# A decoder block with 32 experts on one core: expert weights fetched in 4 MB transfers, 32 KB a partition, in place of 2 MB ones

## Chip, core and metric

The kernel runs on 1 core of a Trainium2 chip. The metric is device time in microseconds (us). Before the change, three runs took 1339.52 us (median), 1335.58 and 1339.84 us.

## What is computed

A block of 256 tokens of 1024 float32 features passes two mixers (a state-space scan and a sparse attention), a merge and a projection, and then a layer of 32 experts, of which each token uses its best four. The kernel computes all of it in float32. Cut to what matters here:

```python
def moe_ffn(h, router_w, router_b, w_gate_up, b_gate_up, w_down, b_down):
    t = h.reshape(256, 1024)
    combine = ...                                  # 256 x 32, four nonzero a row
    out = jnp.zeros_like(t)
    for e in range(32):
        a = clamped_swiglu(t @ w_gate_up[e] + b_gate_up[e])     # 1024 x 2048, 8 MB
        out = out + combine[:, e:e + 1] * (a @ w_down[e] + b_down[e])   # 1024 x 1024, 4 MB
    return out
```

An expert has 12 MB of weights, all 32 have 384 MB (402.65 million bytes), and each byte is read once.

## The kernel before

The first 400 us compute the mixers, the projection and the router. Their weights pass through the first four 8 KB slots of a tile `ring`; when they are done, the whole of `ring` (12 slots of 8 KB a partition) goes to the experts.

**The experts on TensorE.** For every expert the tokens that chose it (64 places) are gathered, multiplied by the gate and up weights, activated, turned, multiplied by the down weights and added back. Two experts make a pair, and two pairs a pass of the loop `Fori`. `odd_half` and `even_half` (L1099, L1122) write out the order of one half each:

- `gather(n)` (L1026 to L1035): for two experts at once, 8 blocks of 128 features by 2 halves of the tokens, with a 128x128 piece of the tile `H2` as the stationary operand and the selection matrix `SPR` as the moving one. Each float32 matmul is two records in the trace, so that a gather has 32 (line L1032). There is one gather a pair, 16 in all.
- `gate_up(s, j, slot, loads_n)` (L1037): unit j of 4 of the gate and up weights, 256 rows, 2 MB. It waits for its transfer and counts `unit_done` at its end. Its matmuls are 16 records at L1043.
- `act_turned(n)` (L1061): four 128x128 transposes of the activations `ABU` (name `HT` in the trace, since it lies in that tile; line L711). 32 in all, one an expert.
- `down(j, slot, loads_n)` (L1048): unit j of 2 of the down weights, 512 rows, 2 MB, 16 records at L1057.
- `combine(n, s)` (L1076, matmuls at L1083) spreads the results back over the tokens, `bias(s)` (L1014) starts an accumulation, and `weights_turned` turns the combining weights (L711, `QT`), once a pair.

The order is G(e+1), then D(e): down of an expert follows gate and up of the next. After G(31) and D(30) there is no more to overlap with: the kernel ends with `combine`, `act_turned` for expert 31, its two down units, `combine`, a norm and the store.

Which rows of a weight matrix a partition holds is fixed by the transfer. A unit of 256 rows goes in as `(p k) n -> p (k n)` with k=2: partition p gets rows 2p and 2p+1, one run of 16 KB. TensorE must therefore take the features of `H2` in the same order, every second one, and so it does in the stationary operand:

```python
first = 256 * (k // 2) + k % 2
ins = mm(bank(5 + k // 4, P, off=P * (k % 4)), H2[:, t, first:first + 255:2],
         SPR[:, t].rearrange("p a b -> p (a b)"), start=(t == 0), stop=(t == T - 1))
```

`act_turned` takes every second column of `ABU` likewise.

**The transfers.** SyncE's queue (SP) issues all of them, in the order of use, through `load_gu` (L501) and `load_dn`. There are 8 places of 16 KB a partition (`places`, L283): two outside `ring` (`slot0`, `slot1`), six in it. A ninth, `once`, is used for one unit alone. A place is loaded again when the unit in it has been multiplied: SP waits for `unit_done`. The first eight or nine transfers are issued one by one as the memory comes free from the mixers (L531 to L547); from then on each waits for the place that the unit 8 before it had.

Of the kernel before, what the change touches and what calls it, by code (L numbers as in the profile page):

```python
# [33 lines left out]
P = 128  # L34
D = 1024
# [18 lines left out]
BIG = 2 * SLOT  # L54
SLOTS = 8
# [3 lines left out]
ONCE = SLOTS  # L59
FIRST_SLOT = (0, 1, 2, ONCE)  # L60
LOOP_SLOT = tuple((n + 3) % SLOTS for n in range(PERIOD))
# [115 lines left out]
def hybrid_block(nc, x, mix_norm_w, w_in, conv_w, conv_b, dt_bias, a_log, d_skip, ssm_norm_w,  # L177
# [3 lines left out]
    with ExitStack() as ctx:  # L181
# [21 lines left out]
        def at_place(name, shape, place, dt=F32R):  # L203
# [149 lines left out]
        slot_full = [sem(f"slot_full{i}") for i in range(SLOTS + 1)]  # L353
# [93 lines left out]
        def loop_loads(i, pos):  # L447

            slot = LOOP_SLOT[pos]
            before = LOOP_SLOT[:pos].count(slot) + FIRST_SLOT.count(slot)  # L450
            return i * (16 * LOOP_SLOT.count(slot)) + 16 * (before + 1)
# [10 lines left out]
        def _(sp):  # L462
# [38 lines left out]
            def load_gu(e, j, slot):  # L501

                src = w_gate_up[0, e, 256 * j:256 * j + 256, :].rearrange("(p k) n -> p (k n)", k=2)
                sp.dma_start(places[slot], src).then_inc(slot_full[slot], 16)

            def load_dn(e, j, slot):

                src = w_down[0, e, 512 * j:512 * j + 512, :].rearrange("(p k) n -> p (k n)", k=4)
                sp.dma_start(places[slot], src).then_inc(slot_full[slot], 16)

            def load_at(pos, e, nxt, slot):

                h, n = pos // PAIR, pos % PAIR
                if n < 4:
                    load_gu(e + (2 * h + 1), n, slot)
                elif n < 6:
                    load_dn(e + 2 * h, n - 4, slot)
                elif n < 10:
                    load_gu(nxt if h else e + 2, n - 6, slot)
                else:  # L520
                    load_dn(e + (2 * h + 1), n - 10, slot)

            def first_load(n):

                if n < GU_U:
                    load_gu(0, n, FIRST_SLOT[n])
                else:
                    load_at(n - GU_U, 0, 4, LOOP_SLOT[n - GU_U])

            sp.wait_ge(pv_read, 16)  # L530
            first_load(0)  # L531
            sp.wait_ge(unit_done, at_unit[("bs", 3)] + 1)
            first_load(1)
            sp.wait_ge(unit_done, at_unit[("bn", 3)] + 1)
            first_load(2)
            low_ready(sp, len(SPLIT_UNITS) - 3)
            low_ready(sp, len(SPLIT_UNITS) - 2)
            first_load(4)
            sp.wait_ge(unit_done, at_unit[("wo", 1)] + 1)
            first_load(5)  # L540
            low_ready(sp, len(SPLIT_UNITS) - 4)
            low_ready(sp, len(SPLIT_UNITS) - 1)
            first_load(6)
# [17 lines left out]
            for n, pos in enumerate((*range(PAIR + 6), PERIOD - 2, PERIOD - 1)):  # L561
                sp.wait_ge(unit_done, units_to(last * 2, n - SLOTS + 1))
                load_at(pos, EXPERTS - 4, 0, LOOP_SLOT[n])
# [143 lines left out]
        def _(pe):  # L707
# [329 lines left out]
            def gate_up(s, j, slot, loads_n):  # L1037

                pe.wait_ge(slot_full[slot], loads_n)
                w = places[slot]  # L1040
# [7 lines left out]
            def down(j, slot, loads_n):  # L1048

                pe.wait_ge(slot_full[slot], loads_n)  # L1050
                w = places[slot]
                for hf in range(2):
                    for k in range(2):
                        lhs = ATS[:, 2 * j + k, 64 * hf:64 * hf + 64]
                        for h in range(2):
                            at = 2048 * k + 1024 * hf + 512 * h
                            ins = mm(psum[64 * h:64 * h + 64, 2, :], lhs, w[:, at:at + 512],  # L1057
                                     start=(j + hf + k == 0), stop=(j == 1 and hf + k == 2))
# [29 lines left out]
            for j in range(GU_U):  # L1088
                pe.wait_ge(xte_ready, 1 if j < 2 else 2)
                gate_up(0, j, FIRST_SLOT[j], 16)  # L1090
# [879 lines left out]
```

## Time and profile before

| | us |
|---|---|
| three runs | 1335.58, 1339.52, 1339.84 |
| the profiled execution, its own time | 1334.48 |
| its span in the trace | 1332.8 |
| TensorE busy | 1234.6 (93%) |
| chain that ended last, transfers of expert weights | 31% of the span |
| a 2 MB expert transfer, from issue to landing | about 34 |

The profile lists for every engine its records with start and length. "PE" are the matmuls of TensorE, "PEld" its loads of the stationary operand, which overlap the matmuls. "Busy" counts overlapping records once. The chain of waits goes back from the last instruction to what released it each time; a row in it that names DMA means that the work after it waited for a transfer. The granted clock of TensorE is 1.00 (2.4 GHz) in all of the expert stage behind its first microseconds.

### The profile page before, as it was taken

Reading aid. Unit: us, or ns where it says so; the run is one execution under the profiler, and the core shown is the slowest. Engines: PE = TensorE matmul, PEld = TensorE weight load, DVE = VectorE, ACT = ScalarE, POOL = GpSimd, SP = SyncE. Lnnn points to the kernel's source line nnn. Section 1 sums busy time; section 2 is a strip of 40 time slices with the busy share of each in tenths; the row PEclk is TensorE's granted clock in tenths of the full one; section 3 lists DMA queues with packets and bytes.
Section 4 is the critical chain, followed back from the end, with each engine's and each line's share of the span. In section 5 each row is a group of like instructions: output and inputs, shape, how many; then the busy total and the mean of one; then the engine's idle time right before and its main releaser. Section 6 shows DMA issues by size and latency. Waiting matters only on the chain.

```text
span 1332.8 us, 17482 instructions
## 1 busy us (share of the span) xinstructions
PE 1234.6 (93%) x7089; PEld 661.9 (50%) x7089; DVE 444.1 (33%) x902; ACT 282.3 (21%) x507; POOL 149.0 (11%) x101
## 2 busy tenths in 40 slices
PE   7999996898899999999999898998989899898985
PEld 7999986777884443434434233332423333232321
DVE  6965446455633131221212213121221212122113
ACT  4673444453331010101101011010101001010001
POOL 1301345353630000000000000000000000000000
PEclk9999997899999999999999999999999999999998
DMA  7747433112698999999999999999999999999994
GB/s 239 209 129 228 127 106 116 64 64 95 236 363 342 395 432 426 430 427 430 427 430 427 428 428 428 430 427 430 427 430 427 431 427 430 427 428 429 426 428 205
DMA packets 79964, 454.08 MB, mean 341 GB/s; under 512 B 10160, under 2 KB 53296, under 8 KB 55344
## 3 DMA queue, kind: packets, MB, share of 16 engines
q1 hardware_dynamic: 76960, 451.30, 82.9%
q10 hardware_dynamic: 2960, 2.17, 0.6%
q8 instruction: 31, 0.51, 0.2%
q14 instruction: 13, 0.11, 0.0%
HBM read 452.40 MB, written 1.05 MB: 340 GB/s over the span
## 4 chain that ended last, share of the span: by engine, by line
PE 60%; DMA 31%; DVE 6%; ACT 1%; issue 1%; ACTq 1%; POOL 0%; DVEq 0%; SPq 0%
DMA ring<-in_w_gate_up_dram 28%; PE psum L1043 19%; PE psum L1057 10%; PE psum L757 9%; PE psum L760 7%; PE psum L1032 5%; PE psum L1083 3%; DMA ring<-in_w_down_dram 3%; PE psum L711 2%; DVE AMX L1754 1%; PE psum L930 1%; DVE YV L1706 1%; DVE WL L1472 1%; PE psum L967 1%; PE psum L1014 1%
## 5 line engine op out<-in xcount | busy, mean ns | idle before, releaser
L1043 PE MATMUL psum<-ring,ZS 128*64 128x512 f32 x1504 | 355.2, 616 | 14.2 <-DMA ring<-in_w_gate_up_dram 14.2
L1043 PEld LDWEIGHTS psum<-ring,ZS 128*64 128x64 f32 x1504 | 100.0, 134 | 230.3 <-issue 192.5
L1906 DVE TENSOR_TENSOR X<-X,psum 128x1024 f32<-128x1024 f32 x64 | 75.3, 1217 | 388.7 <-PE psum L1083 388.7
L1057 PE MATMUL psum<-ring,HT 128*64 128x512 f32 x784 | 176.6, 596 | 20.3 <-DMA ring<-in_w_down_dram 19.6
L1890 DVE TENSOR_SCALAR ZS<-psum 128x512 f32<-128x512 f32 x32 | 22.1, 692 | 315.1 <-PE psum L1043 315.1
L1043 PE MATMUL psum<-slot,ZS 128*64 128x512 f32 x528 | 123.8, 615 | 2.0 <-DMA slot<-in_w_gate_up_dram 2.0
L1057 PEld LDWEIGHTS psum<-ring,HT 128*64 128x64 f32 x784 | 54.4, 136 | 129.9 <-issue 104.0
L1391 ACT ACTIVATE HT<-psum 128x512 f32<-128x512 f32 x32 | 19.1, 597 | 324.3 <-PE psum L711 324.3
L1472 DVE TENSOR_TENSOR WL<-ring,WH 128x2048 fp32r<-128x2048 f32 (+1 forms) x30 | 71.2, 2377 | 46.0 <-ACT WH L1184 46.0
L1184 ACT ACTIVATE WH<-ring 128x2048 fp32r<-128x2048 f32 (+1 forms) x42 | 78.5, 1873 | 10.2 <-issue 6.1
L1043 PEld LDWEIGHTS psum<-slot,ZS 128*64 128x64 f32 x528 | 35.6, 134 | 73.3 <-issue 64.7
L1032 PEld LDWEIGHTS psum<-QT,XC 128*128 128x128 f32 x512 | 63.0, 200 | 14.4 <-issue 14.4
L1032 PE MATMUL psum<-QT,XC 128*128 128x128 f32 x512 | 66.0, 289 | 1.5 <-DVEq L1829 1.5
L1083 PE MATMUL psum<-HT,QT 64*128 64x512 f32 x264 | 65.6, 615 | 1.6 <-ACT HT L1395 1.6
L1395 ACT ACTIVATE HT<-psum 128x512 f32<-128x512 f32 x32 | 19.1, 597 | 222.3 <-PE psum L1057 222.3
L621 POOL TENSOR_TENSOR WL<-ring,WH 128x2048 fp32r<-128x2048 f32 x12 | 55.2, 4603 | 41.2 <-ACT WH L1184 41.2
L1057 PE MATMUL psum<-slot,HT 128*64 128x512 f32 x240 | 54.3, 594 | 5.8 <-DMA slot<-in_w_down_dram 5.8
L1387 ACT ACTIVATE ZS<-ZS 128x512 f32<-128x512 f32 x32 | 20.2, 630 | 136.0 <-DVE ZS L1890 136.0
L757 PE MATMUL psum<-HTH,WH 128*128 128x256 f32 x320 | 47.5, 292 | 0.0
L757 PE MATMUL psum<-HTL,WH 128*128 128x256 f32 x320 | 46.2, 287 | 0.3 <-DVE HTL L1485 0.3
L757 PE MATMUL psum<-HTH,WL 128*128 128x256 f32 x320 | 45.4, 285 | 0.0
L1083 PEld LDWEIGHTS psum<-HT,QT 64*128 64x128 f32 x264 | 22.7, 186 | 45.4 <-issue 45.4
(322 smaller groups left out, 1306.6 us busy)
## 6 DMA issues: line engine op xcount, KB each, us to landing
ring<-in_w_gate_up_dram SPq DMA_DIRECT2D x94, 2048.0 KB, 33.8
ring<-in_w_down_dram SPq DMA_DIRECT2D x49, 2048.0 KB, 35.1
slot<-in_w_gate_up_dram SPq DMA_DIRECT2D x33, 2048.0 KB, 33.7
ring<-in_w_in_dram SPq DMA_DIRECT2D x30, 1024.0 KB, 5.5
slot<-in_w_down_dram SPq DMA_DIRECT2D x15, 2048.0 KB, 35.0
ring<-in_w_branch_ssm_dram SPq DMA_DIRECT2D x4, 1024.0 KB, 4.9
ring<-in_w_branch_nsa_dram SPq DMA_DIRECT2D x4, 1024.0 KB, 5.0
ring<-in_w_out_dram SPq DMA_DIRECT2D x4, 1024.0 KB, 4.9
```

The source lines that it names most:

```text
L621: g.tensor_tensor(WL[i % SPLITS][:], slot_view(k, SLOT), WHF[i % SPLITS], ALU.subtract).then_inc(wl_pool, 1)
L711: return nc.tensor.transpose(o, i, IDN[:, :])
L757: ins = mm(bank(b, 2, SEQ)[:, half], w[:, k, rows], src[:, k, :], start=(n == 0 and k == 0), stop=(n == 2 and k == KT - 1))
L760: ins = mm(bank(b, 2, nco)[:, half], src[:, k, rows], w[:, k, :], start=(n == 0 and k == 0), stop=(n == 2 and k == KT - 1))
L1032: ins = mm(bank(5 + k // 4, P, off=P * (k % 4)), H2[:, t, first:first + 255:2], SPR[:, t].rearrange("p a b -> p (a b)"), start=(t == 0), s ...
L1043: ins = mm(psum[64 * (c % 2):64 * (c % 2) + 64, c // 2, :], XTS[:, k, s], every_other_pair(w[:, 2048 * (k % 2):2048 * (k % 2) + 2048], c), ...
L1057: ins = mm(psum[64 * h:64 * h + 64, 2, :], lhs, w[:, at:at + 512], start=(j + hf + k == 0), stop=(j == 1 and hf + k == 2))
L1083: ins = mm(psum[:, 3 + 2 * t + h, :], CTS[r, s, t], YSB[r, :], start=True, stop=True)
L1184: a(WH[i % SPLITS][:, 0:n], slot_view(u, n), ACT.Copy).then_inc(wh_ready, 1)
L1472: v.tensor_tensor(WL[i % SPLITS][:, 0:n], slot_view(u, n), WHF[i % SPLITS][:, 0:n], ALU.subtract).then_inc(wl_ready, 1)
L1890: v.tensor_scalar(GBU.rearrange("p (q f) -> p q f", q=2), gu[:, :, :, 0], 7.0, None, ALU.min).then_inc(g_ready, 1)
L1906: v.tensor_tensor(xo, xo, psum[:, 3 + 2 * t:5 + 2 * t, :], ALU.add).then_inc(o_read, 1)
```

## The change

Two units become one transfer: 512 rows of gate and up weights, or all 1024 rows of a down matrix, each 4 MB, with 32 KB in one run for a partition (k=4 and k=8 in `(p k) n -> p (k n)`). The eight places of 16 KB become four of 32 KB on the same bytes. TensorE still works unit by unit and counts `unit_done` for each, but waits for a transfer ahead of every second unit, and SP waits with a transfer until both units of the old content are done. The first transfers, which go into memory that comes free piece by piece, and the down weights of the last expert stay 2 MB (`load_half`). Of the first ones, the transfer into `once` now goes ahead of one into the last free half place, and what was the first half of D(0) there is the first loaded half of G(2).

Since a partition now holds four neighbouring rows of gate and up weights, `gather` takes every fourth feature of `H2`; since it holds eight of the down weights, `act_turned` takes every fourth column of `ABU`.

```diff
-BIG = 2 * SLOT
-SLOTS = 8
+BIG = 4 * SLOT
+HALF = BIG // 2
+SLOTS = 4
-FIRST_SLOT = (0, 1, 2, ONCE)
-LOOP_SLOT = tuple((n + 3) % SLOTS for n in range(PERIOD))
+UNITS_4 = PERIOD // 2
+FIRST_SLOT = (0,)
+LOOP_SLOT = tuple((n + 2) % SLOTS for n in range(UNITS_4))
...
-        places = [at_place("slot0", [P, BIG], xdt_at + 4 * D, F32)[:],
-                  at_place("slot1", [P, BIG], ec_at, F32)[:]]
-        places += [part(ring, i * SLOT, BIG) for i in (4, 2, 8, 0, 10, 6)]
-        places += [at_place("once", [P, BIG], xc_at + 4 * 2048, F32)[:]]
+        places = [at_place("slot0", [P, BIG], xdt_at + 4 * D, F32)[:]]
+        places += [part(ring, i * SLOT, BIG) for i in (4, 0, 8)]
+        once = at_place("once", [P, HALF], xc_at + 4 * 2048, F32)[:]
...
+            def gate_up_rows(e, ab):
+
+                return w_gate_up[0, e, 512 * ab:512 * ab + 512, :].rearrange("(p k) n -> p (k n)", k=4)
+
+            def down_rows(e):
+
+                return w_down[0, e].rearrange("(p k) n -> p (k n)", k=8)
+
+            def load_half(rows, hi, to, full):
+
+                sp.dma_start(to, rows[:, HALF * hi:HALF * hi + HALF]).then_inc(full, 16)
...
             sp.wait_ge(unit_done, at_unit[("wo", 2)] + 1)
-            first_load(7)
-            sp.wait_ge(unit_done, NU)
-            first_load(8)
+            load_half(gate_up_rows(1, 1), 1, half_place(3, 1), slot_full[3])
             sp.wait_ge(bias_ready, 1)
             sp.wait_ge(rt_full, 1)
             sp.wait_ge(h2_ready, 4)
-            first_load(3)
-            for n in range(9, GU_U + PERIOD):
-                before = max(q for q in range(n) if (FIRST_SLOT + LOOP_SLOT)[q] == (FIRST_SLOT + LOOP_SLOT)[n])
-                sp.wait_ge(unit_done, NU + before + 1)
-                first_load(n)
+            load_half(gate_up_rows(0, 1), 1, once, part_full["once"])
+            sp.wait_ge(unit_done, NU)
+            load_half(gate_up_rows(2, 0), 1, half_place(1, 1), part_full["G2a"])
+            sp.wait_ge(unit_done, NU + 1)
+            load_half(down_rows(0), 0, half_place(0, 0), part_full["D0"])
+            sp.wait_ge(unit_done, NU + 2)
+            load_half(down_rows(0), 1, half_place(0, 1), slot_full[0])
+            sp.wait_ge(unit_done, NU + 3)
+            load_half(gate_up_rows(2, 0), 0, half_place(1, 0), slot_full[1])
+            sp.wait_ge(unit_done, NU + 5)
+            load_half(gate_up_rows(2, 1), 0, half_place(2, 0), slot_full[2])
...
+            for unit in range(5, UNITS_4):
+                sp.wait_ge(unit_done, units_to(0, 2 * unit - 6))
+                load_at(unit, 0, 4, LOOP_SLOT[unit])
             last = rounds(sp)
             with sp.Fori(1, last) as i:
-                for pos in range(PERIOD):
-                    sp.wait_ge(unit_done, units_to(i * 2, pos - SLOTS + 1))
-                    load_at(pos, (i % EX4) * 4, ((i + 1) % EX4) * 4, LOOP_SLOT[pos])
+                for unit in range(UNITS_4):
+                    sp.wait_ge(unit_done, units_to(i * 2, 2 * unit - 6))
+                    load_at(unit, (i % EX4) * 4, ((i + 1) % EX4) * 4, LOOP_SLOT[unit])
...
+            for hi in range(2):
+                sp.wait_ge(unit_done, units_to(last * 2, 11 + hi))
+                load_half(down_rows(EXPERTS - 1), hi, half_place(LOOP_SLOT[9], hi),
+                          slot_full[LOOP_SLOT[9]] if hi else part_full["last"])
...
                 for k in range(KT):
                     for t in range(T):
-                        first = 256 * (k // 2) + k % 2
-                        ins = mm(bank(5 + k // 4, P, off=P * (k % 4)), H2[:, t, first:first + 255:2],
+                        first = 512 * (k // 4) + k % 4
+                        ins = mm(bank(5 + k // 4, P, off=P * (k % 4)), H2[:, t, first:first + 509:4],
                                  SPR[:, t].rearrange("p a b -> p (a b)"), start=(t == 0), stop=(t == T - 1))
...
                 w = places[slot]
-                for hf in range(2):
-                    for k in range(2):
-                        lhs = ATS[:, 2 * j + k, 64 * hf:64 * hf + 64]
-                        for h in range(2):
-                            at = 2048 * k + 1024 * hf + 512 * h
+                for k in range(4 * j, 4 * j + 4):
+                    lhs = ATS[:, k // 2, 64 * (k % 2):64 * (k % 2) + 64]
+                    for h in range(2):
+                        at = 1024 * k + 512 * h
...
                 for jb in range(4):
-                    first = 256 * (jb // 2) + jb % 2
-                    ins = tr(bank(7, 4, P)[:, jb], ABU[:, first:first + 255:2])
+                    ins = tr(bank(7, 4, P)[:, jb], ABU[:, jb:jb + 509:4])
                 ins.then_inc(at_full, 1)
```

SP's instructions at the start of the expert transfers, before (`ring` stands for six of the places; a row ending in x5 is five alike):

```order
L504 DMA slot0_62<-in_w_gate_up_dram 128x4096
L504 DMA slot1_63<-in_w_gate_up_dram 128x4096
L504 DMA ring<-in_w_gate_up_dram 128x4096 x5
L509 DMA ring<-in_w_down_dram 128x4096
L504 DMA once_64<-in_w_gate_up_dram 128x4096
L509 DMA slot0_62<-in_w_down_dram 128x4096
L504 DMA slot1_63<-in_w_gate_up_dram 128x4096
L504 DMA ring<-in_w_gate_up_dram 128x4096 x3
L509 DMA ring<-in_w_down_dram 128x4096 x2
```

and the same place of the change:

```order
L513 DMA slot0_62<-in_w_gate_up_dram 128x4096 x2
L513 DMA ring<-in_w_gate_up_dram 128x4096 x5
L513 DMA once_63<-in_w_gate_up_dram 128x4096
L513 DMA ring<-in_w_gate_up_dram 128x4096
L513 DMA slot0_62<-in_w_down_dram 128x4096 x2
L513 DMA ring<-in_w_gate_up_dram 128x4096 x3
L530 DMA ring<-in_w_down_dram 128x8192
```

Fourteen transfers of 4096 floats a partition come first in both; the two of D(1), last in the first list, are one of 8192 floats in the second, and from there on all are.

SP's last expert transfers, before (G(31) unit 3, D(30) in two, D(31) in two):

```order
L504 DMA ring<-in_w_gate_up_dram 128x4096
L562 REGISTER_ALU
L509 DMA ring<-in_w_down_dram 128x4096
L562 REGISTER_ALU
L509 DMA ring<-in_w_down_dram 128x4096
L562 REGISTER_ALU
L509 DMA ring<-in_w_down_dram 128x4096
L562 REGISTER_ALU
L509 DMA ring<-in_w_down_dram 128x4096
```

and in the change:

```order
L530 DMA ring<-in_w_gate_up_dram 128x8192
L573 REGISTER_ALU
L530 DMA ring<-in_w_down_dram 128x8192
L576 REGISTER_ALU
L513 DMA ring<-in_w_down_dram 128x4096
L576 REGISTER_ALU
L513 DMA ring<-in_w_down_dram 128x4096
```

D(30) lands in one piece now, D(31) still in two.

## Rows read from the trace of the kernel before

**Rows 1.** The page: transfers in 40 slices of the span.

```profile
DMA  7747433112698999999999999999999999999994
GB/s 239 209 129 228 127 106 116 64 64 95 236 363 342 395 432 426 430 427 430 427 430 427 428 428 428 430 427 430 427 430 427 431 427 430 427 428 429 426 428 205
```

**Rows 2.** Chain of waits in order of time: start us, us, what.

```profile
400.73 5.49 PE psum L1032 x32
406.23 7.35 PE psum L1043 x32
...
458.17 7.35 PE psum L1043 x32
...
495.19 3.96 PE psum L1032 x32
499.16 7.02 PE psum L1057 x32
...
620.09 7.35 PE psum L1043 x32
...
674.07 3.78 PE psum L1043 x16
678.00 30.84 DMA ring<-in_w_gate_up_dram
...
729.66 3.78 PE psum L1043 x16
733.59 33.98 DMA ring<-in_w_gate_up_dram
...
788.40 3.78 PE psum L1043 x16
```

**Rows 3.** Timeline of TensorE's matmuls in the last experts: start us, us, what, idle before.

```profile
1258.17 7.58 PE L1043 MATMUL psum<-ring,ZS 128*64 128x512 f32 x32
...
1305.96 3.65 PE L1057 MATMUL psum<-ring,HT 128*64 128x512 f32 x16 [1.15 <-DMA ring<-in_w_down_dram]
```

**Rows 4.** Queries by line: TensorE's operand loads, record length in ns min/median/max, first and last start.

```profile
L840 PEld LDWEIGHTS psum<-XC x16: 190/191/192, 97.4 to 154.2; 128*128 128x128 f32 x16
...
L1032 PEld LDWEIGHTS psum<-QT,XC x512: 193/196/332, 400.7 to 1244.9; 128*128 128x128 f32 x171
...
L711 PEld LDWEIGHTS psum<-IDN,HT x128: 194/209/219, 436.7 to 1312.7; 128*128 128x128 f32 x128
L711 PEld LDWEIGHTS psum<-IDN,QT x64: 137/140/143, 428.8 to 1287.4; 128*128 128x128 f32 x64
...
L1043 PEld LDWEIGHTS psum<-slot,ZS x176: 133/134/137, 406.2 to 671.1; 128*64 128x64 f32 x176
...
L809 PEld LDWEIGHTS psum<-ring,EC x32: 195/213/218, 92.0 to 95.7; 128*64 128x64 f32 x32
```

**Rows 5.** Timeline of operand loads: two neighbouring loads of L809, then a turning, a gather.

```profile
92.46 0.21 PEld L809 LDWEIGHTS psum<-ring,EC 128*64 128x64 f32 x1
92.58 0.21 PEld L809 LDWEIGHTS psum<-ring,EC 128*64 128x64 f32 x1
...
436.72 0.56 PEld L711 LDWEIGHTS psum<-IDN,HT 128*128 128x128 f32 x4 [0.85 <-issue]
...
441.15 3.84 PEld L1032 LDWEIGHTS psum<-QT,XC 128*128 128x128 f32 x32 [0.85 <-issue]
```

**Rows 6.** By windows: stretch, us; PE, PEld, DVE, ACT, POOL busy; clock; DMA share; GB/s.

```profile
100.00:109.00 9.00, 9.00 (x79) 9.00 (x78) 4.92 (x9) 3.71 (x4) 1.98 (x2) 1.00 1.10 350
520.00:1300.00 780.00, 740.63 (x3514) 272.79 (x3512) 167.44 (x318) 73.75 (x122) 0.00 (x0) 1.00 1.01 428
```

**Rows 7.** Timeline of SP's queue: the two transfers of D(1), start us and us.

```profile
436.83 4.75 SPq L509 DMA_DIRECT2D ring<-in_w_down_dram  x2
```

More of the change, by code:

```diff
@@ L58 @@
 PERIOD = 2 * PAIR
-ONCE = SLOTS
-FIRST_SLOT = (0, 1, 2, ONCE)
-LOOP_SLOT = tuple((n + 3) % SLOTS for n in range(PERIOD))
+UNITS_4 = PERIOD // 2
+FIRST_SLOT = (0,)
+LOOP_SLOT = tuple((n + 2) % SLOTS for n in range(UNITS_4))
+PARTS = ("G0a", "G0b", "once", "G1a", "G1b", "D0", "G2a", "G2b", "last")
 OFF_Z, OFF_XBC, OFF_DT, OFF_Q = 0, 1024, 3072, 3088
@@ L352, in hybrid_block @@
         ring_full = [sem(f"ring_full{i}") for i in range(STREAM)]
-        slot_full = [sem(f"slot_full{i}") for i in range(SLOTS + 1)]
+        slot_full = [sem(f"slot_full{i}") for i in range(SLOTS)]
+        part_full = {n: sem(f"part_full_{n}") for n in PARTS}
         unit_done = sem("unit_done")
@@ L445, in units_to, with loop_loads @@
             return pair * PAIR + (NU + GU_U + n)
-        def loop_loads(i, pos):
-            slot = LOOP_SLOT[pos]
-            before = LOOP_SLOT[:pos].count(slot) + FIRST_SLOT.count(slot)
+        def loop_loads(i, unit):
+            slot = LOOP_SLOT[unit]
+            before = LOOP_SLOT[:unit].count(slot) + FIRST_SLOT.count(slot)
             return i * (16 * LOOP_SLOT.count(slot)) + 16 * (before + 1)
@@ new lines, in half_place, with load_at @@
+            def half_place(slot, hi):
+                return places[slot][:, HALF * hi:HALF * hi + HALF]
+            def load_at(unit, e, nxt, slot):
+                h, n = unit // 6, unit % 6
+                if n < 2:
+                    rows = gate_up_rows(e + (2 * h + 1), n)
+                elif n == 2:
+                    rows = down_rows(e + 2 * h)
+                elif n < 5:
+                    rows = gate_up_rows(nxt if h else e + 2, n - 3)
+                else:
+                    rows = down_rows(e + (2 * h + 1))
+                sp.dma_start(places[slot], rows).then_inc(slot_full[slot], 16)
@@ new lines, in _ @@
+            sp.wait_ge(unit_done, NU + 1)
[5 more added lines that the diff above has]
+            sp.wait_ge(unit_done, NU + 5)
+            load_half(gate_up_rows(2, 1), 0, half_place(2, 0), part_full["G2b"])
+            sp.wait_ge(unit_done, NU + 6)
@@ L561, in _ @@
-            for n, pos in enumerate((*range(PAIR + 6), PERIOD - 2, PERIOD - 1)):
-                sp.wait_ge(unit_done, units_to(last * 2, n - SLOTS + 1))
-                load_at(pos, EXPERTS - 4, 0, LOOP_SLOT[n])
+                for unit in range(UNITS_4):
+                    sp.wait_ge(unit_done, units_to(i * 2, 2 * unit - 6))
+                    load_at(unit, (i % EX4) * 4, ((i + 1) % EX4) * 4, LOOP_SLOT[unit])
+            for unit in range(9):
+                sp.wait_ge(unit_done, units_to(last * 2, 2 * unit - 6))
+                load_at(unit, EXPERTS - 4, 0, LOOP_SLOT[unit])
@@ L1035, in gather, with gate_up @@
                         ins.then_inc(xte_full, 1)
-            def gate_up(s, j, slot, loads_n):
-                pe.wait_ge(slot_full[slot], loads_n)
-                w = places[slot]
+            def gate_up(s, j, slot, loads_n=None, early=None, w=None):
+                if early:
+                    pe.wait_ge(part_full[early], 16)
+                if loads_n is not None:
+                    pe.wait_ge(slot_full[slot], loads_n)
+                if w is None:
+                    w = places[slot][:, HALF * (j % 2):HALF * (j % 2) + HALF]
                 for k in (2 * j, 2 * j + 1):
@@ L1089, in _ @@
                 pe.wait_ge(xte_ready, 1 if j < 2 else 2)
-                gate_up(0, j, FIRST_SLOT[j], 16)
+                if j == 0:
+                    gate_up(0, 0, 0, None, "G0a")
+                elif j == 1:
+                    gate_up(0, 1, 0, 16)
+                elif j == 2:
+                    gate_up(0, 2, 1, None, "G0b")
+                else:
+                    gate_up(0, 3, 1, None, "once", once)
                 if j == 1:
@@ L1118, in odd_half, with even_half @@
                 pe.wait_ge(at_ready, pair * 2 + 1)
-                for j in range(DN_U):
-                    down(j, *at(4 + j))
-            def even_half(pair, i, pos):
-                def at(n):
-                    return LOOP_SLOT[pos + n], loop_loads(i, pos + n)
+                down(0, LOOP_SLOT[d], loop_loads(i, d), early[2])
+                down(1, LOOP_SLOT[d])
+            def even_half(pair, i, unit, early=(None, None)):
+                a, b, d = unit + 3, unit + 4, unit + 5
                 pe.wait_ge(gu_read, pair * 2 + 2)
@@ L1151, in _ @@
             pe.wait_ge(at_ready, last * 4 + 4)
-            for j in range(DN_U):
-                down(j, LOOP_SLOT[PAIR + 6 + j], loop_loads(last, PAIR + 6 + j))
+            down(0, LOOP_SLOT[9], None, "last")
+            down(1, LOOP_SLOT[9], loop_loads(last, 9))
             combine(last * 4 + 4, 1)
```

79 lines of the change are left out of this document (31 added, 48 removed).

## The prediction

> **What bounds the kernel now.** I read the page's slices first. From about 470 us to 1300, the transfers run at 426 to 432 GB/s slice after slice [rows 1], so the stream of expert weights looks like the limit. The chain of waits says when it becomes so. Up to 674 us the chain is TensorE alone. From 678 us on it returns to a transfer of gate weights once a pair [rows 2]. The periods give both prices: with TensorE as the limit, a pair of experts takes 674.07 - 620.09 = 53.98 us; with transfers as the limit 788.40 - 729.66 = 58.74 us [rows 2]. So TensorE starts late, with a full store of weights, catches up at 674 us and from then on has 4.76 us to spare a pair. The time ends with the later of two paths: the transfers, or TensorE's own work. The change touches both, and I price each.
>
> How much TensorE can grow before it sets the end is the sum of its waits for transfers. From 674.07 to 1258.17 us, the same place of the order ten pairs later [rows 2, 3], 584.1 us passed, and ten pairs of its own work are 539.8: 44.3 us of waiting. From 1258.17 to the last down unit of expert 30 at 1305.96 [rows 3] 47.8 us passed. The same stretch without waits is 458.17 to 499.16, plus half of the 7.02 us of down, less the 3.96 us gather, which the last half has not [rows 2]: 40.5 us. That is 7.3 us more. **Slack: 51.6 us.**
>
> **The change, path of TensorE.** The number of its matmuls, their widths and the layout of what moves are as before. What differs is that the stationary operand of `gather` and of `act_turned` is read with a step of four floats (16 bytes) instead of two. The trace of before has no load with step four, so I bound it by its neighbours [rows 4]. For 128 columns of float32: 191 ns contiguous, 196 ns at step two (the gather). For 64 columns: 134 ns contiguous (L1043), 213 ns at step eight (L809, where `KCP` is read with `j=8`). For the transposes, whose loads run faster: 140 ns contiguous, 209 ns at step two. From 64 to 128 contiguous columns a load grows by 57 ns, which leaves about 78 ns that don't depend on columns. Then L809 spends 135 ns on 64 columns, 2.1 ns on each, and the transposes at step two 131 ns on 128 columns, 2.05 ns on each two, and contiguously 62 ns, 1.94 ns on each four. Four columns side by side, two at step two and one at step eight have in common that they take one piece of 16 bytes. So 16 bytes of a partition cost about 2 ns or a little more, whatever is used of them, and the gather at step two just fits within its normal pace. At step four every column has its own 16 bytes, as at step eight: 128 columns take 270 ns plus 78, about 345 ns a load. That is a reading of three rows, not a measurement; the two ends are no growth (the step two of the gather cost 5 ns) and the full step eight. A gain I exclude: no row has a wider step that is shorter.
>
> Advanced Engine Details and Errata, a page of the Trainium skill, states in Memory Cachelines that SBUF lines have 16 bytes and that two hits on a line are wanted to hide its latency, with a penalty for another line at each access. By that rule, step two is free and step four is not; the gather's 196 ns agrees, the transposes' 209 ns at step two does not quite, and the page gives no price.
>
> Loads overlap matmuls, so what counts is how closely they follow each other. In the gather 32 loads take 3.84 us [rows 5]: (3.84 - 0.196)/31 = 0.118 us apart; the matmuls of the gather, 3.96 us, keep the same pace. The loads of L809 with 64 columns follow each other at 0.12 us [rows 5], a little below their 0.135. For 128 columns that is 0.24 us apart, at most 0.27. A gather then grows by 32 x (0.24 - 0.124) = 3.7 to 32 x (0.27 - 0.124) = 4.7 us. I take 3.9, near the spacing that was measured. **16 gathers: 62.4 us** (ends 0 and 75).
>
> A turning has four such loads, 0.56 us in all [rows 5], 0.117 apart. At step four the first is 0.13 longer, and the others follow at 0.24 instead of 0.117, some of which the matmuls hide today: 0.42 us (ends 0 and 0.5). **32 turnings: 13.4 us**, all on TensorE's path, since its next matmuls stand behind them.
>
> Together 75.8 us, against 51.6 of slack. **TensorE becomes the limit, and the end moves by 75.8 - 51.6 = 24.2 us.** Its period would be 53.98 + 3.9 + 0.84 = 58.7 us a pair from the first pair on.
>
> **The change, path of the transfers.** (a) *Packets.* Expert runs of 16 KB move at 428 GB/s [rows 1, 6], 26.75 by each of 16 DMA engines: 612 ns a run. The 1 KB runs of the mixers' weights move at 350 GB/s [rows 6]: 46.8 ns a run. The straight line through both has 9.1 ns a run plus 0.0368 ns a byte. A run of 32 KB would take 1215 ns instead of 2 x 612: 9.1 ns saved. An engine carries 8 runs of each transfer, and from D(1) on there are 88 transfers of 4 MB (192 units of 2 MB, less the first 14 and the last two, is 176): 88 x 8 x 9.1 ns = 6.4 us saved. Ends: 0 (long runs cut or no cheaper), and twice as much, 12.8 us.
>
> DMA: Bandwidth & Descriptors, a page of the Trainium skill, gives in Why small descriptors are slow about 3 cycles of the 850 MHz fabric a packet, 3.5 ns. By the page the gain would be an estimated 2.5 us in place of 6.4; the 9.1 ns of the rows decide.
>
> (b) *Coarser release.* D(1) was issued in two, at 436.83 us and 4.4 us later [rows 7]; now both wait for the second, and G(3) likewise. At that time the queue is short of work (slices of 395 GB/s ahead of the steady 427 [rows 1]), so this is not hidden: 3 us lost, ends 0 and 4.4. Later, three places stay queued behind the one in use, some 29 us of transfers against a hold of 8, which covers it. (c) *Earlier entries.* `once` ahead of the last half place leaves the same nine transfers landed before TensorE's first release: 0. (d) *The end.* D(30) lands whole where its first half was used 4.8 us earlier: 3.65 us more behind the landing if transfers set the end [rows 3]. G(31) b is done by then. (e) SP has half the instructions, on no path: 0. (f) The first gather lies ahead of the first release, so its growth delays the transfers too.
>
> Without slower loads that is 3.0 - 6.4 + 3.65 = +0.3 us: nothing. With them, +4.6 (3.9 by (f), 0.4 by the last turning), far under the 24.2 of TensorE's path, which is thus the later and the answer. The wait that goes is TensorE's for transfers; what is late next is TensorE's `unit_done` for SP, and the queue will show gaps.
>
> **The sum.** The profiled execution took 1334.48 us (1332.8 of span and 1.7 around it); plus 24.2 is 1358.7. The median of the runs, 1339.52, stands 5.0 above it, and with the same step it becomes **1363.7 us**. Ends of this case: 16 x 3.7 + 32 x 0.4 - 51.6 = 20.4, and 16 x 4.7 + 32 x 0.5 - 51.6 = 39.6, so 1360 to 1379; and down to 1350 if the loads pipeline better than at L809.
>
> **Rivals.** (1) *Loads at step four cost no more than at step two.* For: 196 against 191 ns in the gather. Against: 213 against 134 at step eight and 209 against 140 in the transposes. Then transfers stay the limit, +0.3 us: 1339.8, within the bound. (2) *Step four is harmless and long runs bring more than the line through two rows says*: all overhead goes, 12.8 us saved, and the sum is 3.0 - 12.8 + 3.65 = -6.1: 1333.4, **faster**. For: steady slices of up to 431 or 432 among 426 [rows 1], so the ceiling isn't 428. Against: the line's own slope. It decides once a 4 MB transfer takes under 9.67 us, with the gather under 5 us. (3) *The change doesn't do what it says*: runs of 32 KB are cut into two of 16 KB on their way, no gain, and +6.65 remains: 1346.2, slower. Nothing in this trace is longer than 16 KB, so no row excludes it. It changes nothing while TensorE is the limit.
>
> **Chances.** Forecast 0.77; rival 1 0.11; rival 2 0.07; rival 3, or a partly slower gather under transfers as the limit, 0.05. A difference of 0.3%, 4 us, is about what a measurement of this kernel can tell. Faster 0.07, within it 0.11, slower 0.82. The range takes the forecast's own, rival 3 and rival 1: 1338 to 1379.
>
> **What would show it.** In the profile after: L1032's loads near 345 ns and a gather near 7.9 us; the transposes' loads near 340 ns; a period of 58 to 60 us a pair already between 460 and 700 us; TensorE's waits for transfers nearly gone and slices of transfers below 428 with a rest at the end; and packets of 32 KB, in 104 expert transfers instead of 192. I am wrong if the gather stays near 4 us: then the chain will still end in transfers, and the time tells rival 1 from 2 and 3 by the rate in GB/s of the steady slices (431, 435, 428).

## The result, and the profile after

The change is slower. Nine runs of each kernel have medians of 1336.59 us before (1332.35 to 1339.84) and 1343.04 us after (1341.78 to 1345.72); the ratio is 1.0055, with a 95% interval of 1.0042 to 1.0068, so some 7.3 us (5.6 to 9.1; the medians lie 6.5 apart). The forecast was 24.2 us more: the sign was right, the size three times too large. The profiled execution after took 1344.44 us, with a span of 1342.7. TensorE's mean granted clock over the span is 0.980, before it was 0.981, so the clock is not the cause.

The page of the kernel after: its transfers by slices, their packets, its chain, and the gather's loads among the costliest groups:

```profile
DMA  7737433212688799999999999999999999999993
GB/s 239 212 110 238 127 104 117 64 64 94 235 340 334 313 420 426 432 432 433 429 434 432 430 433 432 430 433 430 433 433 430 431 435 429 432 433 429 433 428 161
DMA packets 67291, 454.07 MB, mean 338 GB/s; under 512 B 8752, under 2 KB 51888, under 8 KB 53936
...
PE 88%; DVE 6%; DMA 2%; ACT 2%; issue 1%; ACTq 1%; POOL 0%; DVEq 0%
...
L1047 PEld LDWEIGHTS psum<-QT,XC 128*128 128x128 f32 x512 | 120.7, 329 | 14.4 <-issue 14.4
```

In the chain, transfers had 31% of the span before and have 2% now: TensorE sets the time. Most of the steady slices rose from 427 to 430 GB/s to 430 to 433 [rows 1], so the long runs did become cheaper; the fourteenth slice (436 to 470 us after, 433 to 466 before) fell from 395 to 313.

The chain of waits of the kernel after, in order of time (start us, us, what):

```profile
446.58 7.66 PE psum L1047 x32
...
1254.38 7.66 PE psum L1047 x32
...
1286.86 25.51 DMA ring<-in_w_down_dram
1312.51 7.10 PE psum L1078 x32
```

The gather, 3.96 us before [rows 2], takes 7.66. A pair takes 57.70 us from the second gather to the last, (1254.38 - 446.58)/14, where TensorE alone needed 53.98 [rows 2]: 3.72 us more, which is the gather and nothing else. Not once does the chain go to a transfer of expert weights before 1286.86, and there only just, as the timeline of TensorE's matmuls shows (start us, us, what, idle before):

```profile
403.88 7.70 PE L1047 MATMUL psum<-QT,XC 128*128 128x128 f32 x32 [1.50 <-DVEq L1852]
...
1312.51 7.09 PE L1078 MATMUL psum<-ring,HT 128*64 128x512 f32 x32 [0.43 <-DMA ring<-in_w_down_dram]
```

The two paths meet within 0.43 us at D(30). The operand loads of the two lines that the change touches, in the queries by line (ns min/median/max, first and last start):

```profile
L1047 PEld LDWEIGHTS psum<-QT,XC x512: 308/330/331, 403.8 to 1261.5; 128*128 128x128 f32 x171
...
L726 PEld LDWEIGHTS psum<-IDN,HT x128: 195/212/222, 442.1 to 1322.6; 128*128 128x128 f32 x128
```

and the timeline of the loads of a turning (one `act_turned`, four transposes) and of a gather:

```profile
442.08 0.56 PEld L726 LDWEIGHTS psum<-IDN,HT 128*128 128x128 f32 x4 [0.85 <-issue]
...
446.51 7.54 PEld L1047 LDWEIGHTS psum<-QT,XC 128*128 128x128 f32 x32 [0.85 <-issue]
```

The gather's loads went from 196 to 330 ns and follow each other at (7.54 - 0.33)/31 = 0.233 us. The transposes' loads stayed: 212 ns after 209, four of them in 0.56 us as before [rows 4, 5].

**The difference as a sum.** From the start of the first gather to the end of D(30)'s matmuls the execution before needed 1305.96 + 3.65 - 400.73 = 908.9 us [rows 2, 3], after 1312.51 + 7.09 - 403.88 = 915.7: 6.8 more. TensorE's work gives 15 x 3.70 = 55.5, and 7.70 - 5.49 = 2.2 for the first gather; with the 51.6 of slack gone and 0.43 of waiting left, that is 57.7 - 51.6 + 0.4 = 6.5. The spans differ by 9.9, since in this execution the first gather began 3.15 us later. That start moves between kernels whose mixers are alike (400.73 before, 406.83 in gather4_in_before below), so I compare traces from the first gather on.

A small part of the later start does belong to the change. From GpSimd's fourth write of `H2` to the first gather it is 6.44 us before (394.29 to 400.73) and 6.43 in gather4_in_before, but 6.85 after (397.03 to 403.88); there ScalarE's two transfer issues ahead of the router's root take 0.80 and 0.68 us, before 0.44 and 0.43. With these 0.4 us the traces give 7.2 of the 7.3 us that the runs show.

### The profile page after: what moved, and what is told of

It is laid out like the page before. It is cut to its first block, busy times and chain, and to the rows that moved or that the text cites. A ratio compares the mean times of both kernels' runs of the same rounds, so it can differ in the third digit from the quotient of the medians.

```text
span 1342.7 us, 17182 instructions
## 1 busy us (share of the span) xinstructions
PE 1281.9 (95%) x7089; PEld 719.0 (54%) x7089; DVE 444.9 (33%) x902; ACT 281.9 (21%) x507; POOL 148.9 (11%) x101
## 3 DMA queue, kind: packets, MB, share of 16 engines
q1 hardware_dynamic: 64288, 451.30, 81.7%
HBM read 452.40 MB, written 1.05 MB: 338 GB/s over the span
## 4 chain that ended last, share of the span: by engine, by line
PE 88%; DVE 6%; DMA 2%; ACT 2%; issue 1%; ACTq 1%; POOL 0%; DVEq 0%
PE psum L1062 34%; PE psum L1078 16%; PE psum L1047 9%; PE psum L772 9%; PE psum L775 7%; PE psum L1103 5%; PE psum L726 3%; DMA ring<-in_w_down_dram 2%; DVE AMX L1777 1%; PE psum L1029 1%; PE psum L945 1%; DVE YV L1729 1%; DVE WL L1495 1%; PE psum L982 1%; PE psum L853 1%
## 5 line engine op out<-in xcount | busy, mean ns | idle before, releaser
L1078 PE MATMUL psum<-ring,HT 128*64 128x512 f32 x768 | 169.2, 593 | 1.1 <-ACT HT L1414 0.7
L1047 PEld LDWEIGHTS psum<-QT,XC 128*128 128x128 f32 x512 | 120.7, 329 | 14.4 <-issue 14.4
L1047 PE MATMUL psum<-QT,XC 128*128 128x128 f32 x512 | 123.7, 402 | 1.5 <-DVEq L1852 1.5
L636 POOL TENSOR_TENSOR WL<-ring,WH 128x2048 fp32r<-128x2048 f32 x12 | 55.5, 4622 | 40.8 <-ACT WH L1207 40.8
```

What stands on the lines that cost most here:

```text
L636: g.tensor_tensor(WL[i % SPLITS][:], slot_view(k, SLOT), WHF[i % SPLITS], ALU.subtract).then_inc(wl_pool, 1)
```

## Experiments

**gather2_in_after**: the kernel after with the gather's old step.

```diff
-                        first = 512 * (k // 4) + k % 4
-                        ins = mm(bank(5 + k // 4, P, off=P * (k % 4)), H2[:, t, first:first + 509:4],
+                        first = 256 * (k // 2) + k % 2
+                        ins = mm(bank(5 + k // 4, P, off=P * (k % 4)), H2[:, t, first:first + 255:2],
```

> The changed kernel with one thing taken back: the gather reads H2 with a step of two floats again (its rows then meet the wrong weights; amount and order of all work stay). Theory A, the gather alone carries the loss through TensorE's path: L1047's loads fall from 330 to 196 ns, a gather from 7.66 to about 3.97 us, TensorE catches the transfers up near 670 to 700 us, behind that a pair takes 6 x 9.72 = 58.3 us, and the end lies 0.3 us from the kernel before (ratio 0.998 to 1.002). Theory B, the coarser release and the later first use of D(30) carry it: the time stays 5 to 7 us above the kernel before (ratio 1.004 to 1.005), whatever the gather takes.

Median 1337.84 us, ratio 1.001 (0.9997 to 1.0023). The gather's loads by line:

```profile
L1047 PEld LDWEIGHTS psum<-QT,XC x512: 193/196/336, 406.4 to 1254.8; 128*128 128x128 f32 x171
```

and its chain of waits:

```profile
1064.62 7.35 PE psum L1062 x32
...
1076.40 3.97 PE psum L1047 x32
...
1087.64 27.27 DMA ring<-in_w_gate_up_dram
1114.96 5.43 PE psum L1062 x16
...
1122.89 7.35 PE psum L1062 x32
```

One step in an index took the loss away, as far as the interval can tell, and the chain returns to transfers. A pair now takes 1122.89 - 1064.62 = 58.27 us, against 58.74 before [rows 2]. The prediction's line through two kinds of runs gives 6 x 8 x 9.1 ns = 0.44 less a pair, 58.30. (The 5.43 us row is taken up in the last section.)

**gather4_in_before**: the other way round, the step of four alone in the kernel before.

```diff
-                        first = 256 * (k // 2) + k % 2
-                        ins = mm(bank(5 + k // 4, P, off=P * (k % 4)), H2[:, t, first:first + 255:2],
+                        first = 512 * (k // 4) + k % 4
+                        ins = mm(bank(5 + k // 4, P, off=P * (k % 4)), H2[:, t, first:first + 509:4],
```

> The kernel before with the gather's step of four floats alone (its rows meet the wrong weights). Theory A: loads of 330 ns, gathers of 7.66 us, a pair 57.7 us from the start to nearly the end; 15 x 3.7 + 2.2 = 57.7 us of work more against 51.6 us of slack, so 6 us slower, ratio 1.0045, with 1.003 to 1.006 as bounds. Theory B, 3.7 us a pair vanish in the 4.76 us that TensorE has to spare while transfers set the pace: 0 to 2 us slower, ratio 1.000 to 1.002.

Median 1344.65 us, ratio 1.005 (1.0035 to 1.0065): with 2 MB transfers, eight places and the old order of everything, the same loss. Its chain of waits:

```profile
1141.59 7.66 PE psum L1032 x32
...
1199.26 7.66 PE psum L1032 x32
```

57.67 us a pair, with no transfer of expert weights in the chain. So the gather alone is enough to make the loss, and by gather2_in_after it is needed for it.

**turn1_in_after**: the turnings read contiguous columns, the rest as after.

```diff
-                    ins = tr(bank(7, 4, P)[:, jb], ABU[:, jb:jb + 509:4])
+                    ins = tr(bank(7, 4, P)[:, jb], ABU[:, P * jb:P * jb + P])
```

> The changed kernel with act_turned reading ABU contiguously in place of a step of four (its activations meet the wrong weights). Theory A, the step makes the transposes' loads long, but two and four cost the same: the loads fall from 212 to 140 ns, a turning from 0.75 to about 0.62 us, and as TensorE's path sets the end, the span falls by 32 x 0.1 = 3 us. Theory B, the record has its length from something else (the operand's place, or what stands ahead of it): 205 to 215 ns again and a span within 1.5 us.

One run: 1343.14 us. The turnings' loads by line:

```profile
L726 PEld LDWEIGHTS psum<-IDN,HT x128: 137/140/143, 441.4 to 1321.4; 128*128 128x128 f32 x128
```

and the timeline of its last turning but one and of D(30):

```profile
1305.37 0.66 PE L726 MATMUL psum<-IDN,HT 128*128 128x128 f32 x4
1305.96 3.82 PE L1062 MATMUL psum<-ring,ZS 128*64 128x512 f32 x16
1311.30 7.09 PE L1078 MATMUL psum<-ring,HT 128*64 128x512 f32 x32 [1.52 <-DMA ring<-in_w_down_dram]
```

The loads go from 212 to 140 ns, but a turning only from 0.75 to 0.66 us, and D(30) then waits 1.52 us in place of 0.43: with TensorE a little quicker, the transfers set the end at once. From the start of the first gather (403.24) to the end of D(30)'s matmuls it takes 915.15 us, 0.6 less than after, where the expectation had 3. Of a single run the total time decides nothing; these rows do.

**h2_turned**: GpSimd writes `H2` with its columns in the order in which the gather wants them, so that the gather reads contiguous columns; the full result.

```diff
-                g.tensor_tensor(H2[:, :, cols], X[:, :, cols], WFF[:, cols].unsqueeze(1).to_broadcast([P, T, 256]),
+                to = H2[:, :, 512 * (m // 2):512 * (m // 2) + 512].rearrange("p t (k i) -> p t k i", k=4)
+                g.tensor_tensor(to[:, :, :, 64 * (m % 2):64 * (m % 2) + 64],
+                                X[:, :, cols].rearrange("p t (i k) -> p t k i", k=4),
...
+                        ins = mm(bank(5 + k // 4, P, off=P * (k % 4)), H2[:, t, P * k:P * k + P],
```

> The changed kernel, but GpSimd writes H2 in the order in which the gather reads it (four features apart come to lie side by side), so that the gather reads contiguously; the result is the full one. Theory A: loads of about 191 ns, gathers of 3.8 to 4.0 us, GpSimd's four writes at L709 longer than 1.3 us by up to 2 us each, hidden; ratio to the kernel before 0.998 to 1.001. Theory B (release and end carry the loss): ratio 1.004 or more. A rival inside A: GpSimd's writes are so slow that the first gather waits for them, and every microsecond of that is seen at the end.

Median 1339.21 us, ratio 1.002 (1.0009 to 1.0032): most of the loss is gone, not all, and the expected 0.998 to 1.001 is just missed. GpSimd's write and the gather's loads by line:

```profile
L710 POOL TENSOR_TENSOR XC<-X,YV x4: 2112/2122/2123, 378.5 to 398.9; 128x512 f32<-128x512 f32 x4
...
L1050 PEld LDWEIGHTS psum<-QT,XC x512: 186/192/334, 406.0 to 1252.7; 128*128 128x128 f32 x171
```

The permuted write takes 2.12 us against 1.29 before. GpSimd has time for three of the four; the last is not hidden. Beside it VectorE's TENSOR_SCALAR on `ss` (L1813), a step of the router, takes 1.04 us where it took 0.20 before (L1787), and ends at 401.01 us with the write (400.99); from the start of that write to the first gather it is 7.11 us, before 6.44 and in the kernel after 6.85. The gather's loads take 192 ns. The first gather and D(30), in the chain of waits:

```profile
405.99 6.40 PE psum L1050 x32
...
1278.39 30.52 DMA ring<-in_w_down_dram
1309.05 7.10 PE psum L1081 x32
```

From the end of the first gather to the end of D(30) it needs 1309.05 + 7.10 - 412.39 = 903.8 us, the kernel before 1309.61 - 406.22 = 903.4: 0.4 more, where the prediction has +0.3 for the transfers without slow loads. The first gather itself took 6.40 us against 5.49: in windows of 1 us the granted clock stands at 0.50 for its first 5 us, before for 3. With the 0.7 us ahead of it that is 2.0 of the 2.7 us that the ratio gives (1.2 to 4.3 by its interval).

**Halves, first set.** Four kernels put single 4 MB transfers back into two of 2 MB, each half with its own wait and its own release, always in this form:

```diff
+                sp.wait_ge(unit_done, units_to(last * 2, 9 + hi))
+                load_half(down_rows(EXPERTS - 2), hi, half_place(LOOP_SLOT[8], hi),
+                          slot_full[LOOP_SLOT[8]] if hi else part_full["D30"])
```

h2_turned_d30_halved does so for D(30), h2_turned_early_halved for D(1) and G(3)a, h2_turned_ends_halved for all three, and early_halved_in_after for D(1) and G(3)a with the slow gather.

h2_turned_d30_halved, expected:

> h2_turned with the down weights of expert 30 in two transfers of 2 MB, the second half's unit waiting for the second. Theory A, with the quick gather the transfers set the end, so that term (d) shows: 1.4 us of wait ahead of both down units go and the first unit is done before the last landing, 3.5 us less than h2_turned, ratio to the kernel before 0.998 to 1.001. Theory B, the granted clock is what costs: after the pause of 2.1 us once a pair TensorE runs at half its clock for some 3 us, and near the end this sets the time; then the halves gain under 1.5 us.

h2_turned_early_halved, expected:

> h2_turned with D(1) and the first half of G(3) in transfers of 2 MB, each issued when its own half place is free. Theory A, transfers set the end and term (b) shows: the rate between 440 and 470 us rises from 361 to 400 GB/s or more, all later landings come 3 us sooner, ratio to the kernel before 0.998 to 1.001. Theory B, the gaps of that time are made good later in the store: no change against h2_turned, 1.002.

h2_turned_ends_halved, expected:

> Both: D(1), the first half of G(3) and D(30) in halves, H2 turned by GpSimd. Theory A: both gains add, 6 to 6.5 us below h2_turned, that is ratio 0.996 to 0.998 to the kernel before, so that 4 MB transfers win by what their longer runs save. Theory B: at most one of the two shows, ratio 0.999 to 1.001.

early_halved_in_after, expected:

> The changed kernel, its slow gather kept, with D(1) and the first half of G(3) in halves. Theory A, TensorE's path sets its end with the transfers at most 1 us behind: within 1 us of the changed kernel, ratio to the kernel before 1.004 to 1.006, while the wait ahead of D(30) goes from 0.4 us to none. Theory B, the late release is what made the changed kernel slow: 3 us or more less, ratio 1.003 or under.

| kernel | median us (before 1336.90) | ratio (95%) |
|---|---|---|
| h2_turned_d30_halved | 1337.70 | 1.0007 (0.9991 to 1.0022) |
| h2_turned_early_halved | 1337.46 | 1.0004 (0.9990 to 1.0019) |
| h2_turned_ends_halved | 1337.15 | 1.0003 (0.9990 to 1.0016) |
| early_halved_in_after | 1343.11 | 1.0046 (1.0029 to 1.0063) |

The first two lie within their expected ratios, but gain less than was expected. From the end of the first gather to the end of D(30) h2_turned_d30_halved needs 901.9 us (1302.45 + 7.03 - 407.58), 1.9 less than h2_turned and not 3.5. h2_turned_early_halved has 363 GB/s from 440 to 470 us, h2_turned 361, where 400 or more were expected. The last kernel keeps the loss, as expected, though D(30) still waits 0.22 us where no wait was expected. That the coarse release is not the cause of the loss follows from gather4_in_before, which has the loss with the old release; this row alone would not show it, since the gap may only have moved. The third missed its expectation of 0.996 to 0.998, and the traces say why, twice. At the end, the timeline of h2_turned_d30_halved:

```profile
1284.51 3.82 PE L1069 MATMUL psum<-slot,ZS 128*64 128x512 f32 x16 [2.09 <-DMA slot<-in_w_gate_up_dram]
...
1302.45 7.03 PE L1085 MATMUL psum<-ring,HT 128*64 128x512 f32 x32
```

D(30) no longer waits, so the end hangs on TensorE's run from the landing of G(31), which is whole and late too. At the start, SP's queue in h2_turned_ends_halved (start us, us, what):

```profile
439.42 4.76 SPq L513 DMA_DIRECT2D ring<-in_w_down_dram  x2
451.20 3.76 SPq L513 DMA_DIRECT2D slot<-in_w_gate_up_dram  x2
464.36 0.33 SPq L530 DMA_DIRECT2D ring<-in_w_gate_up_dram  x1
```

The next whole transfer waits for two units, until 464.36: the gap has moved to it.

**Halves, second set.** So h2_turned_last3_halved halves G(31)a, G(31)b and D(30), and h2_turned_both_ends7_halved also D(1), G(3)a, G(3)b and D(2).

h2_turned_last3_halved, expected:

> h2_turned with the last three 4 MB transfers (gate and up weights of expert 31, down of 30) in halves, each unit waiting for its own. h2_turned_d30_halved showed that without a wait at D(30) TensorE's run from the landing of G(31)'s first 4 MB sets the end. Theory A, so it does: with all of expert 31 in halves the run between the last expert landing and the end of the span is 16.8 us as in the kernel before (19.8 in h2_turned, 18.0 with D(30) alone); ratio to the kernel before 0.999 to 1.001. Theory B, the granted clock at the end costs it whatever the halves: 18 us or more again.

h2_turned_both_ends7_halved, expected:

> In halves: D(1), both parts of G(3) and D(2) at the start, G(31) and D(30) at the end; all else 4 MB. In h2_turned_ends_halved the queue ran dry ahead of G(3)'s second part instead of D(1). Theory A, the release costs until the store is large enough: from the end of the first gather to the eighteenth 2 MB landed it takes 56 to 58 us as in the kernel before (56.3; 60.3 in h2_turned), the tail is 16.8 us, and the longer runs' gain is left: 3 to 5 us under the kernel before, ratio 0.996 to 0.998. Theory B: the gap moves on to the next whole transfer once more, ratio 0.998 to 1.000.

Against 1337.42 us of before on the same chip, the first has a median of 1334.89, ratio 0.9984 (0.9970 to 0.9998), the second **1331.11, ratio 0.9948 (0.9930 to 0.9966)**: faster than both kernels. The last byte of the experts lands 18.0 us ahead of the end of the span in both, before 18.2, in h2_turned_d30_halved 20.0 and in h2_turned 21.5 (read in windows of 0.25 us): halves at the end restore the old tail. The timeline of h2_turned_both_ends7_halved, of TensorE and of SP's queue:

```profile
403.88 6.18 PE L1060 MATMUL psum<-QT,XC 128*128 128x128 f32 x32 [1.50 <-DVEq L1865]
...
1304.07 3.65 PE L1091 MATMUL psum<-ring,HT 128*64 128x512 f32 x16 [0.41 <-DMA ring<-in_w_down_dram]
...
460.01 6.00 SPq L513 DMA_DIRECT2D ring<-in_w_gate_up_dram  x2
469.28 4.76 SPq L513 DMA_DIRECT2D ring<-in_w_down_dram  x2
480.58 0.33 SPq L530 DMA_DIRECT2D ring<-in_w_gate_up_dram  x1
```

and its windows (stretch us; PE, PEld, DVE, ACT, POOL busy; clock; DMA share; GB/s):

```profile
520.00:700.00 180.00, 176.94 (x850) 65.65 (x846) 40.16 (x76) 18.15 (x30) 0.00 (x0) 1.00 1.00 432
700.00:1300.00 600.00, 567.99 (x2680) 213.72 (x2682) 127.34 (x242) 55.60 (x92) 0.00 (x0) 0.99 1.00 431
```

It prices the packets: its first gather ended at 410.06, so the second half of D(30) landed 894.0 us behind it, before 1305.96 - 406.22 = 899.7: 5.7 us earlier. 81 whole transfers by 8 by 9.1 ns are 5.9. The period, free of both ends, says the same: 58.74 - 58.27 = 0.47 a pair, or 9.8 ns a run; over nine pairs of before and of this kernel it is 58.73 and 58.29, or 9.2 ns. The timeline of h2_turned_last3_halved, which has the coarse release at the start:

```profile
404.05 5.98 PE L1055 MATMUL psum<-QT,XC 128*128 128x128 f32 x32 [1.50 <-DVEq L1860]
...
1306.63 3.65 PE L1086 MATMUL psum<-ring,HT 128*64 128x512 f32 x16 [0.39 <-DMA ring<-in_w_down_dram]
```

Here the landing comes 1306.63 - 410.03 = 896.6 us behind the first gather, 3.1 earlier than before. The coarse release thus costs 2.6, or 2.9 with the four transfers' own packets.

From the start of the first gather to D(30)'s end the two kernels need 906.2 and 903.8 us, before 908.9. Less the 0.7 us more that pass from GpSimd's last write of `H2` to the first gather, the rows give 2.0 and 4.3 us; the ratios give 2.1 and 7.0 (4.5 to 9.4). The second gain is thus larger than the expected 3 to 5 us, from six runs, and for the rest of it there is no row.

## Why the prediction was right and wrong

**The mechanism held.** TensorE's gather, slowed by operand loads at a step of four floats, used up the slack and took the end from the transfers. Loads: 345 ns forecast, 330 measured; spacing 0.24 and 0.233; gather 7.9 and 7.66. Rival 1 (loads no dearer) fell at the first row. Rival 2 (all overhead gone, faster) fell with both_ends7: the saving is the line's 9 ns a run, not twice as much. Rival 3 (runs cut) fell with the steady 432 GB/s and with the packets: of the 12672 that SP's queue has less on the page (64288 after, 76960 before), 11264 are one for each partition of 88 transfers, which is what uncut runs of 32 KB save. The other 1408 are of under 512 bytes, 16 a transfer. The rule of the Trainium skill (Advanced Engine Details and Errata, Memory Cachelines) that two hits on a line of 16 bytes are wanted agrees with the gather, whose loads take 196 ns with two columns on a line and 330 with one; it doesn't fit the transposes, with 209 and 212. For the cost of a packet the Trainium skill (DMA: Bandwidth & Descriptors, Why small descriptors are slow) gives about 3 cycles, an estimated 3.5 ns; measured are 5.7 us / (81 x 8) = 8.8 ns a run here, which include one short packet for each eight runs that no experiment separates.

**The step that failed** is the second term of TensorE's path, the turnings: "At step four the first is 0.13 longer, and the others follow at 0.24 instead of 0.117 ... 0.42 us", 13.4 us for 32 turnings. It measured 0: four loads in 0.56 us and a turning in 0.75 us in both kernels, the loads 212 ns where near 340 were forecast. The premise was that 16 bytes cost about 2 ns whatever is used of them, also in a transpose. But the transposes' own rows, 140 ns contiguous and 209 at step two, allowed another reading: that a transpose's load pays for any step once. That the step-two load took as long as L809's, 209 and 213 ns for 64 pieces of 16 bytes each, spoke for the premise; the gather's 196 ns for as many pieces did not, so the rows already held two kinds of load. Why a transpose's load stays at 212 ns is open. I used those rows for the rule and never asked what they say against it; the lower end, 0, stood in the text but went into no case of its own.

**The size of the gathers' term** was 62.4 us and measured 57.7: 15 x 3.70 in place of 15 x 3.9, and 2.2 for the first. Before, that one took 5.49 us, more than the 3.96 of the others, since the granted clock stood at 0.50 for its first 3 us; after, it took 7.70 with five of them at 0.50, hardly more than the 7.66 of the others. So it had less to lose. That row stood in [rows 2]; I had not used it.

Both misses add up to 18.1 us of 75.8, a quarter of the added work. They became a factor of three or four because the result is a small difference: 75.8 - 51.6 = 24.2 against 57.7 - 51.6 = 6.1. The slack itself was right, since with it the sum in the section on the result closes to 0.3 us. The forecast of 1363.7 us also stood on a median of three runs, 1339.52; nine runs put it at 1336.59, 2.9 us lower.

**The transfers' path**, forecast at +0.3 without slow loads, measured +0.4 (h2_turned). Its parts: packets -6.4, and -5.7 with 81 of 88; release +3.0, and 2.6 to 2.9. With slow loads it was forecast at +4.6, and at 6.8 here it stood as late as TensorE's: D(30)'s landing is 900.9 us behind the first gather's end (1312.51 - 411.58), in h2_turned 896.7. I counted in (f) the first gather alone. The second, at 446.58, also lies ahead of a release that the short queue waits for. SP issues the transfer behind D(1) 42.6 us after the end of the first gather before (448.81 - 406.22), 46.3 in gather4_in_before (460.88 - 414.54), 45.8 in h2_turned (458.22 - 412.39) and 49.7 after (461.30 - 411.58). So the slow second gather, the only one between these two points, costs 3.75 us with the old release, the coarse release costs 3.2 with a quick gather, and together they cost 7.1. Windows of 10 us of the kernel before:

```profile
440.00:450.00 10.00, 10.00 (x62) 5.73 (x60) 2.67 (x4) 1.82 (x3) 0.00 (x0) 1.00 0.98 413
450.00:460.00 10.00, 10.00 (x50) 3.18 (x48) 2.35 (x2) 0.60 (x1) 0.00 (x0) 1.00 0.97 392
```

and of the kernel after, with both:

```profile
440.00:450.00 10.00, 10.00 (x45) 5.50 (x42) 2.67 (x4) 1.23 (x2) 0.00 (x0) 1.00 0.76 292
450.00:460.00 10.00, 10.00 (x47) 6.11 (x48) 0.00 (x0) 1.19 (x2) 0.00 (x0) 1.00 0.74 318
```

Of the 4.2 us by which D(30) lands later than in h2_turned, 3.9 (49.7 - 45.8) have thus arisen by then. The two paths being so close also says why no single repair won: the gather's gave 1.002, the halves at the start alone 1.0046, and only the gather's repair with halves at both ends brought the gain of the packets out.

## What to carry to other kernels

A transfer's run length sets how rows are interleaved in SBUF, and with it the step of TensorE's operand loads: price each kind of load by its own rows, and reorder once at the write rather than at 16 reads (here the permuted write cost under 1 us, the slow reads 57.7 of TensorE's work). Large transfers pay in the steady stream, small ones at its two ends, where a release is waited for or the last landing is; and all of the waiting ones must be small, or the gap moves to the next. When a path has slack, forecast the sum before the subtraction and its error with it: a quarter of the added work was three quarters of this forecast.

## What the runs showed of the hardware, unexpected

Float32 operand loads of 128 columns: in matmuls 192 ns (contiguous, h2_turned), 196 (step two), 330 (step four); in transposes 140, 209 and 212. A matmul's load pays at step four, a transpose's at step two and no more at four. A gather at step four takes 7.66 us at a granted clock of 1.00 and took 7.70 with five of them at 0.50, while one at step two took 5.49 with three at 0.50 instead of 3.96: the loads at step four set a pace that the clock did not change here.

In all six kernels whose GpSimd permutes `H2`, VectorE's TENSOR_SCALAR beside the fourth write takes 1.04 or 1.05 us instead of 0.20 and ends within 0.05 us of the write.

A pause of TensorE can be followed by a lower clock. In the kernel before no pause in the steady stream was longer than 1.2 us, and the granted clock stood at 1.00. With 4 MB landings and a quick gather the waits for gate weights clump into one of some 2.1 us a pair. The timeline of h2_turned at two of them:

```profile
1056.32 5.43 PE L1065 MATMUL psum<-slot,ZS 128*64 128x512 f32 x16 [2.10 <-DMA slot<-in_w_gate_up_dram]
...
1172.93 3.82 PE L1065 MATMUL psum<-slot,ZS 128*64 128x512 f32 x16 [2.10 <-DMA slot<-in_w_gate_up_dram]
```

and windows of 2 us around the first:

```profile
1056.00:1058.00 2.00, 1.69 (x6) 0.55 (x8) 0.00 (x0) 0.00 (x0) 0.00 (x0) 0.64 0.99 426
1058.00:1060.00 2.00, 2.00 (x8) 0.62 (x6) 0.00 (x0) 0.00 (x0) 0.00 (x0) 0.51 0.99 426
1060.00:1062.00 2.00, 2.00 (x10) 0.59 (x8) 0.00 (x0) 0.00 (x0) 0.00 (x0) 1.00 1.06 459
```

Behind the first pause the granted clock falls to 0.51, the 1.2 GHz level, until about 1060 us, and 16 records take 5.43 us in place of 3.82. Behind an equal pause two pairs later the records take 3.82, and in both_ends7 the pauses of 2.08 us from 992 to 1226 are all followed by 3.82. It comes in blocks: in h2_turned the six pauses from 823 to 1115 are followed by the lower clock, in both_ends7 the four from 701 to 876, the others of that length not. So the pause alone doesn't decide; what does is open. In the steady stream the 1.6 us lie in TensorE's slack, since the wait of some 1.5 us ahead of the next down weights then goes. At the end they can reach the time: in gather2_in_after and h2_turned_early_halved the last such pause, at 1290 and 1289 us, is followed by 5.37 and 5.43, and D(30) then starts without a wait; as it waited 1.42 us in h2_turned, the cost is an estimated 0.2 us.
